# An output projection as three split products, its weights prepared during the recurrence and its low parts streamed in a ring

## The reference

```python
    o = group_rmsnorm(o, norm_g, HGRN_HEADS) * jax.nn.silu(g_out.astype(jnp.float32))   # recurrence
    ...
    return group_rmsnorm(b_gate * y, norm_g, CONV_GROUPS)                               # convolution
    ...
    h = h + jnp.concatenate([y_hgrn, y_conv], axis=-1) @ w_out[l]
    h = h + moe_ffn(rmsnorm(h, norm_ffn_g[l]), ...)
    return rmsnorm(h, norm_final_g)[:, N_META:]
```

## Time and profile before

| | us |
|---|---|
| three runs | 1575.82, 1578.70, 1580.32; median 1578.70 |
| the profiled execution | 1578.89 |
| its span, first to last instruction | 1577.1 |
| TensorE busy | 1492.2 (95%) |
| TensorE weight loads | 1273.3 |
| VectorE busy | 913.8 (58%) |
| GpSimd busy | 844.7 (54%) |
| ScalarE busy | 582.6 (37%) |
| granted TensorE clock, mean | 0.979 |

### The profile page before, as it was taken

How to read it: one execution, slowest core, us unless ns; L and a number is a source line. 1 busy time by engine, 2 the same in 40 slices (tenths; PEclk the granted TensorE clock), 3 DMA queues, 4 the chain that set the end, 5 groups by cost and what they waited for, 6 DMA issues and landing times.

```text
span 1577.1 us, 29085 instructions
## 1 busy us (share of the span) xinstructions
PE 1492.2 (95%) x9554; PEld 1273.3 (81%) x9554; DVE 913.8 (58%) x1595; ACT 582.6 (37%) x1052; POOL 844.7 (54%) x697
## 2 busy tenths in 40 slices
PE   6999999999979999979999999999999999999990
PEld 5799889899834666758999998888998998888980
DVE  3332688788867866344555546555555555555552
ACT  6433545444334321102333333333343333333333
POOL 0332163360601313335667877777777777777761
PEclk9999999999989999989999999999999999999995
DMA  5389521212070011426999999999999999999976
GB/s 189 92 261 299 196 80 31 76 53 80 28 287 27 28 54 54 161 78 246 334 326 339 333 328 325 328 328 344 339 336 326 335 327 325 331 320 340 327 213 229
DMA packets 104441, 356.95 MB, mean 226 GB/s; under 512 B 28151, under 2 KB 38360, under 8 KB 83406
## 3 DMA queue, kind: packets, MB, share of 16 engines
q1 hardware_dynamic: 60622, 246.60, 42.0%
q0 software_dynamic: 43776, 109.80, 26.2%
HBM read 300.68 MB, written 73.91 MB: 238 GB/s over the span
## 4 chain that ended last, share of the span: by engine, by line
PE 49%; DMA 3%; issue 1%; POOL 1%; ACT 0%; DVE 0%; POOLq 0%; SPq 0%; ACTq 0%
PE gu L1713 34%; PE ype L1735 4%; PE yrest L1724 4%; PE ype L1736 3%; PE ype L1737 3%; DMA acc_rows<-YE,sia 1%; DMA acc_rows<-YF,sib 1%; DMA A<-acc_rows 1%; POOL wi L1646 0%; POOL acc_rows L1653 0%; POOL acc_rows L1668 0%; DVE A L1892 0%; SPq L1627 0%; ACT junkf L1832 0%; ACT YF L1789 0%
## 5 line engine op out<-in xcount | busy, mean ns | idle before, releaser
L1646 POOL DMA_INDIRECT wi<-xn_rows,gi x320 | 412.7, 1290 | 117.1 <-issue 97.0
L1852 DVE TENSOR_TENSOR WL<-place,WH 128x2048 fp32r<-128x2048 f32 x65 | 149.1, 2294 | 329.9 <-ACT WH L1780 226.2
L1713 PEld LDWEIGHTS gu<-wi,place 128*128 128x128 f32 x2112 | 290.4, 190 | 5.9 <-issue 3.3
L1713 PE MATMUL gu<-wi,place 128*128 128x160 f32 x2112 | 293.0, 299 | 2.0 <-SPq L1609 1.9
L1713 PE MATMUL gu<-XS,place 128*128 128x160 f32 x2048 | 284.4, 299 | 1.7 <-issue 1.7
L1713 PEld LDWEIGHTS gu<-XS,place 128*128 128x128 f32 x2048 | 281.6, 190 | 5.1 <-issue 2.7
L1131 POOL DMA_INDIRECT slot_table<-pay,si x64 | 62.4, 975 | 170.6 <-DVEq L1440 155.0
L1653 POOL DMA_INDIRECT acc_rows<-YF,sib x65 | 107.1, 1648 | 76.3 <-ACT YF L1789 42.5
L1784 ACT ACTIVATE SS<-gu 128x160 f32<-128x160 f32 x130 | 39.3, 302 | 263.4 <-PE gu L1713 208.9
L1780 ACT ACTIVATE WH<-place 128x2048 fp32r<-128x2048 f32 x65 | 124.2, 1911 | 0.5 <-issue 0.5
L1668 POOL DMA_INDIRECT acc_rows<-YE,sia x65 | 102.8, 1581 | 33.6 <-issue 24.0
(11 more groups left out here) (299 smaller groups left out, 2717.2 us busy)
## 6 DMA issues: line engine op xcount, KB each, us to landing
place<-in_w_gate_e SPq DMA_DIRECT2D x65, 1024.0 KB
place<-in_w_up_e SPq DMA_DIRECT2D x65, 1024.0 KB
place<-in_w_down_e SPq DMA_DIRECT2D x65, 1024.0 KB
place<-in_w_in POOLq DMA_DIRECT2D x16, 512.0 KB, 7.2
late_parts<-wq_parts POOLq DMA_DIRECT2D x8, 1024.0 KB, 6.0
late_parts<-xn_parts POOLq DMA_DIRECT2D x8, 1024.0 KB, 6.0
wf_parts<-late_parts POOLq DMA_DIRECT2D x8, 1024.0 KB, 5.1
w_low<-late_parts POOLq DMA_DIRECT2D x8, 1024.0 KB, 5.2
```

Source lines behind the costliest of these rows:

```text
L1646: pool.indirect_dma_start(XQ[q][:, s * DQ:(s + 1) * DQ], None, quarters_d, bass.IndirectOffsetOnAxis(ap=index[s], axis=0), bounds_check=QU ...
L1713: last = pe.matmul(gu[f][:, k, :], raw[:, t, f * P:f * P + P], XS[q][:, t, :], start=(t == 0), stop=(t == KT - 1))
L1852: tt(WL[q][:, :], WR[q][2][:, :], WH[q][:, :].bitcast(F32), ALU.subtract).then_inc(s_dlo, 1)
```

## The change

`project` multiplies split operands: for each of the four chunks of a part, high rows by high weights, high rows by low weights, low rows by high weights, all in fp32r (three matmuls of 512 columns in the place of one in float32).

*The weights.* They are prepared in the recurrence, one chunk of 128 channels per turn. SyncE loads the chunk (512 KB). ScalarE multiplies it by the norm's gain per channel (`wo_chunk`) and rounds one half of its columns to fp32r behind `decays(3)`, the other behind the copy of the turned keys (`wo_high_part`). GpSimd subtracts (`wo_low_part`): for the first half of chunk 2h ahead of the convolution's first half of head h, for the second half ahead of its second, for chunk 2h + 1 behind the head's last step and at the start of the next head. SyncE stores both parts to DRAM (4 of 256 KB per chunk), and the next chunk's load waits for the subtractions of the one before. The stage's end waits for the last store.

*In the output stage.* The high weights stay in SBUF, loaded in two halves. The low weights come in 128 loads of one chunk and half, 256 KB each, in the order in which `project` uses them (`UNITS`), into a ring of 6 buffers; SyncE issues the first six between the two high halves, and a later one when the product that used its buffer is done. Up to the sixth chunk of the next tile they stand ahead of the wait for a tile's normed rows on SyncE's queue.

*The rows.* `mix` no longer multiplies by the gains. It writes the products into R, ScalarE copies them to fp32r (`conv_high`, `gated_high`), and VectorE subtracts: for the convolution within `mix`, for the recurrence's rows in the new `mixed`, which stands ahead of `residual`. `conv_high` stands behind the squares of the tile after next, `gated_high` behind that tile's roots and the kept transposes.

*Beside that.* The transposed rows xT keep 5 tiles instead of 8, so `keep` waits for the shared expert from tile 5 on; the squares of `row_squares` are written to X2 instead of a buffer of their own, behind waits for its last readers; in the router's tail and in the experts several counting semaphores are merged into one.

```diff
     K.QO = keep("QO", [P, HEADS, T])
+    K.GL, K.QH = (w[:, :, :].rearrange("p t n -> p (t n)").rearrange("p (h t) -> p h t", h=HEADS) for w in (WI0, WI1))
+    split = K.WQ[:, :, :].rearrange("p k n -> p (k n)")
+    K.YH = split[:, 0:HEADS * ALL].rearrange("p (c t) -> p c t", t=ALL)[:, :, META:ALL]
+    at = 2 * HEADS * ALL + 2 * D
+    K.YL = split[:, at:at + D].rearrange("p (i h t) -> p i h t", i=2, h=HEADS)
     K.V = K.place[:, 0:HEADS * ALL].rearrange("p (c t) -> p c t", t=ALL)
...
         tbl_rows = tbl_d.rearrange("(i c) w -> i (c w)", c=CAP)
+        s_ow, s_oh = sem("wo_chunk_in"), sem("wo_chunk_scaled_high")
+        s_ol, s_ost = sem("wo_chunk_low"), sem("wo_chunk_stored")
+        wo_raw, wo_hi, wo_lo = XN[:, 0, :], XP[:, 1, 0:HW], XP[:, 1, HW:2 * HW]
+        gains = K.ng[:, :, :].rearrange("p k h -> p (k h)")
...
+            sp.wait_ge(s_ps[1], 32 * HEADS)
+            for c in range(KT):
+                if c:
+                    sp.wait_ge(s_ol, 2 * c)
+                sp.dma_start(wo_raw, w_out[:, c, :]).then_inc(s_ow, 16)
+                for half in range(2):
+                    sp.wait_ge(s_ol, 2 * c + half + 1)
+                    sp.dma_start(K.wo_high_d[:, c, HW * half:HW * half + HW], wo_hi.bitcast(F32)).then_inc(s_ost, 16)
+                    sp.dma_start(K.wo_low_d[:, half, c, :], wo_lo.bitcast(F32)).then_inc(s_ost, 16)
+            sp.wait_ge(s_ost, 32 + 64 * KT)
...
+
+            def wo_low_part(c, half):
+                pool.wait_ge(s_oh, 3 * c + half + 2)
+                pool.tensor_tensor(wo_lo, wo_raw[:, HW * half:HW * half + HW], wo_hi.bitcast(F32), ALU.subtract).then_inc(s_ol, 1)
...
                 load_parts(h, 2)
+                if h:
+                    wo_low_part(2 * h - 1, 1)
                 for k in range(2):
+                    wo_low_part(2 * h, k)
...
+                wo_low_part(2 * h + 1, 0)
...
             def turn(h, r, ahead):
                 i = h * 2 + r
                 base = h * 10 + (FQ + 6 * r)
+
+                def wo_chunk():
+                    act.wait_ge(s_ow, i * 16 + 16)
+                    act.sem_inc(s_t, 1)
+                    act.activation(wo_raw, wo_raw, ACT.Copy, scale=gains[:, bass.ds(i, 1)]).then_inc(s_oh, 1)
+                    act.wait_ge(s_oh, i * 3 + 1)
+                    act.sem_inc(s_t, 1)
+
+                def wo_high_part(half):
+                    act.wait_ge(s_ost, i * 64 + (32 + 32 * half))
+                    act.sem_inc(s_t, 1)
+                    act.activation(wo_hi, wo_raw[:, HW * half:HW * half + HW], ACT.Copy).then_inc(s_oh, 1)
 
...
                 decays(3)
+                wo_chunk()
+                wo_high_part(0)
...
+                wo_high_part(1)
...
 
+        UNITS = [(half, HEADS * (1 - part) + h) for j in range(TT)
+                 for half, part in (((0, 0), (1, 0), (0, 1), (1, 1)) if j == 0 else ((0, 0), (0, 1), (1, 0), (1, 1)))
+                 for h in range(HEADS)]
+        PER_TILE = 4 * HEADS
...
         @block.sync
         def _(sp):
+            def load_low(u):
+                half, c = UNITS[u]
+                if u >= RING:
+                    sp.wait_ge(s_lu, u - RING + 1)
+                sp.dma_start(K.LO[:, u % RING, :].bitcast(F32), K.wo_low_d[:, half, c, :]).then_inc(s_lw[u % RING], 16)
+
             for k in range(2):
-                sp.dma_start(wo[:, :, 512 * k:512 * k + 512], w_out[:, :, 512 * k:512 * k + 512]).then_inc(s_wo[k], 16)
+                sp.dma_start(WO[:, :, 512 * k:512 * k + 512].bitcast(F32), K.wo_high_d[:, :, 512 * k:512 * k + 512]).then_inc(s_wo[k], 16)
+                if k == 0:
+                    for u in range(RING):
+                        load_low(u)
             sp.dma_start(H[0], x[:, 0, :]).then_inc(s_h[0], 16)
...
             for j in range(TT):
+                for u in range(j * PER_TILE + RING, min((j + 1) * PER_TILE + RING, len(UNITS))):
+                    load_low(u)
...
                         pe.wait_ge(s_wo[half], 16)
-                rows = slice(j * P, j * P + P)
+                rows, cols = slice(j * P, j * P + P), slice(512 * half, 512 * half + 512)
                 for h in range(HEADS):
-                    c, y = (h, K.QO) if part else (HEADS + h, YC)
-                    last = pe.matmul(op[half][:, :], y[:, h, rows], wo[:, c, 512 * half:512 * half + 512],
-                                     start=(part == 0 and h == 0), stop=(part == 1 and h == HEADS - 1))
+                    u = done["chunks"]
+                    c = h if part else HEADS + h
+                    assert UNITS[u] == (half, c)
+                    high = (K.QH if part else K.YH)[:, h, rows]
+                    low = K.GL[:, h, rows] if part else K.YL[:, j % 2, h, :]
+                    pe.matmul(op[half][:, :], high, WO[:, c, cols], start=(part == 0 and h == 0), stop=False)
+                    pe.wait_ge(s_lw[u % RING], 16 * (u // RING + 1))
+                    pe.matmul(op[half][:, :], high, K.LO[:, u % RING, :], start=False, stop=False).then_inc(s_lu, 1)
+                    last = pe.matmul(op[half][:, :], low, WO[:, c, cols], start=False, stop=(part == 1 and h == HEADS - 1))
+                    done["chunks"] += 1
...
+                if j >= KEPT:
+                    act.wait_ge(s_gu, j - KEPT + 1)
                 for k in range(2):
-                    last = act.copy(K.xT[:, 4 * k:4 * k + 4, j * P:j * P + P], td[k][:, :, :])
+                    last = act.copy(xT_of(j)[:, 4 * k:4 * k + 4, :], td[k][:, :, :])
                 last.then_inc(s_e2, 1)
...
-                act.activation(junk, H[j % NH], ACT.Square, accum_out=sh[:, j:j + 1]).then_inc(s_s2, 1)
+                if j >= 2:
+                    act.wait_ge(s_t2, j - 1)
+                    act.wait_ge(s_xw[j % 2], 16 * (j // 2))
+                act.activation(X2[j % 2], H[j % NH], ACT.Square, accum_out=sh[:, j:j + 1]).then_inc(s_s2, 1)
...
 
+            def conv_high(j):
+                act.wait_ge(s_mx, 2 * j + 1)
+                act.activation(K.YH[:, :, j * P:j * P + P], R[j % 2][:, HEADS:2 * HEADS, :], ACT.Copy).then_inc(s_mh, 1)
+
+            def gated_high(j):
+                act.wait_ge(s_mx, 2 * j + 2)
+                act.activation(K.QH[:, :, j * P:j * P + P], R[j % 2][:, 0:HEADS, :], ACT.Copy).then_inc(s_mh, 1)
+
...
             for j in range(TT):
                 if j + 2 < TT:
                     squares(j + 2)
+                if j + 1 < TT:
+                    conv_high(j + 1)
+                if j + 2 < TT:
                     roots(j + 2)
                 if j >= 1:
                     keep(j - 1)
+                if j + 1 < TT:
+                    gated_high(j + 1)
                 row_squares(j)
...
                 step(nc.vector.reciprocal(conv, conv))
-                for h in range(HEADS):
-                    last = stt(YC[:, h, cols], YC[:, h, cols], K.ng[:, 1, h:h + 1], conv[:, h, :], ALU.mult, ALU.mult)
-                last.then_inc(s_y, 1)
+                step(tt(conv, conv, YC[:, :, cols], ALU.mult))
+                dve.sem_inc(s_mx, 1)
                 step(nc.vector.reciprocal(gated, gated))
+                dve.wait_ge(s_mh, 2 * j + 1)
+                if j >= 2:
+                    dve.wait_ge(s_op, 2 * j - 2)
+                tt(K.YL[:, j % 2, :, :], conv, K.YH[:, :, cols].bitcast(F32), ALU.subtract).then_inc(s_y, 1)
                 dve.wait_ge(s_sig, j + 1)
                 step(tt(gated, gated, sg[j % 2], ALU.mult))
-                for h in range(HEADS):
-                    last = stt(G[:, h, cols], G[:, h, cols], K.ng[:, 0, h:h + 1], gated[:, h, :], ALU.mult, ALU.mult)
-                step(last)
-                tt(K.QO[:, :, cols], K.QO[:, :, cols], G[:, :, cols], ALU.mult).then_inc(s_y, 1)
+                step(tt(gated, gated, G[:, :, cols], ALU.mult))
+                step(tt(gated, gated, K.QO[:, :, cols], ALU.mult))
+                dve.sem_inc(s_mx, 1)
+
+            def mixed(j):
+
+                gated, cols = R[j % 2][:, 0:HEADS, :], slice(j * P, j * P + P)
+                dve.wait_ge(s_mh, 2 * j + 2)
+                tt(K.GL[:, :, cols], gated, K.QH[:, :, cols].bitcast(F32), ALU.subtract).then_inc(s_y, 1)
...
                     shared_hidden(j - LAG - 1)
+                if j + 1 < TT:
+                    mixed(j + 1)
...
-                        sp.sem_inc(turn["sp"], 1)
+                        sp.sem_inc(s_turn, 1)
                         sp.wait_ge(s_yr, n - 1)
-                        sp.sem_inc(turn["sp"], 1)
```

109 lines of the change are left out of this document (64 added, 45 removed).

## The result

The changed kernel took 1609.0 us (median of four runs, 1606.8 to 1609.9) beside 1579.1 us of the kernel before: ratio 1.0193, interval 1.0171 to 1.0216, so 30 us slower. The forecast was 1596 (1583 to 1611). Sign and main cause were right; the size was 13 us short, and the stretch from tile 4 to the end, forecast as a gain of 8.3 us, came out as a loss of 4.5.

The account below looks back on a forecast made before the run. TensorE was taken to set the output stage's pace in tiles 4 to 7, VectorE in tiles 1 to 3. Recurrence 4.9, stores 0.5, start 16.4, mix 3.8, products -8.3 make +17.3 on 1578.9: 1596 us, range 1583 to 1611.

Parts of the forecast that it names:

- The named wait: Output stage, tile 0: TensorE idle 12 to 15 us for a DMA of wo_low, clock 0.50 behind it.
- tile 1 to hidden(0): Output stage up to the shared expert's first hidden rows: VectorE's longer mix in tiles 1 to 3, +3.8 us.
- hidden(0) to the end: From the shared expert's first hidden rows on: cheaper products in tiles 4 to 7, less one new wait, -8.3 us.
- The late w_low: Recurrence: GpSimd's subtraction delays each head's convolution and the w_low load queued behind it, +4.9 us over four heads.
- The 0.5 us for the last stores: Recurrence's end: the last chunk's stores end just behind the stage's end, +0.5 us.
- The start: Output stage, tile 0: the seventh low chunk lands behind queued loads, then half clock; tile 1 restarts at 487.8, +16.4 us.
- lies inside this wait: Output stage's start: the first part starts 3.7 us later behind VectorE's second reciprocal, hidden in the seventh chunk's wait.
- Inside a burst of eight the ring keeps up: Output stage: a 0.26 MB low load takes 0.66 us against 0.70 of use per unit, so nothing added.
- about 4 us in tile 1 and 1 in tile 3: Output stage: TensorE stands still because SyncE waits for normed rows; beside VectorE's later chain, so nothing added.
- the ring starves in every tile: Output stage rival: low loads cost SyncE over 1 us each, +7; or VectorE is slowed; 1603 to 1611, chance 0.13.
- The gain of the products: Output stage, tiles 4 to 7: each projection part saves 0.56 us, 9.0 in all, less 0.7: -8.3 us.
- The mix: Output stage, VectorE: 1.5 us more per tile over tiles 1 to 3, less 0.7: +3.8 us; covered in tiles 4 to 7.

Follow-up runs that it names:

- d: Changed kernel with x rows and shared weights issued one at a time between the ring's refills, not ahead of them: 1597.2 us, ratio 1.0118 to the kernel before.
- b: Changed kernel without the output-weight preparation in the recurrence, raw weights standing where the parts would: 1609.1 us, ratio 1.0197 to the kernel before.
- j: h with the second high half issued behind four low units, not ten, and without the weight preparation: 1562.8 us, ratio 0.9973 to the kernel before.
- l: h with the second high half behind four low units and the wait for the last stores at the output stage's head: 1564.3 us, ratio 0.9994.
- c: Changed kernel with one fp32 product of the high parts for the three fp32r products, no low parts loaded: 1595.8 us, ratio 1.0099 to the kernel before.
- g: Changed kernel with d's issue order, e's ring of ten, and ScalarE's roots and keep ahead of conv_high: 1579.7 us, ratio 1.0016 to the kernel before.
- h: g with two low-part subtractions moved on VectorE: tile 0's conv half before the second reciprocal, the next tile's gated half behind the residual: 1575.3 us, ratio 0.9995.
- e: Changed kernel with a ring of ten low units instead of six, xT keeping three tiles instead of five: 1593.4 us, ratio 1.0104 to the kernel before.
- a: Changed kernel loading only the first six low units, products reading whatever lies in their slot: 1584.7 us, ratio 1.0045 to the kernel before.

## Why the prediction was partly right

**Direction and main cause: right.** The named wait came: 14.41 us for a DMA of wo_low in tile 0 (12 to 15 forecast), with the granted clock at 0.54 over the stretch, and tile 1's first product at 492.6 (near 493 forecast). d shows that the backlog makes the wait.

**The sum, term by term.** Forecast against trace, in us:

| step | forecast | measured |
|---|---|---|
| recurrence, to the stage's start | +5.4 | +3.1 in the trace; 2 to 3 by b and j |
| stage's start to tile 1's first product | +16.4 | +18.2 |
| tile 1 to hidden(0) | about +3.8 | +4.4 |
| hidden(0) to the end | about -8.3 | +4.5 |
| sum | +17.3 | +30.2 |

**The late w_low: wrong, 4.9 us too much.** The step "The convolution started at 328.87; now 0.56 + 1.06 + 0.14 + 0.62 + 0.15 + 1.31 + 0.1 behind the decay of 329.69" took the wrong decay. ScalarE's row at 329.69 is two decays behind the one that the new calls follow, which ran at 324.41 in the changed kernel. GpSimd was free by then, so its subtraction was done at 328.8, and TensorE has no wait for w_low in the recurrence of the changed kernel. The 0.5 us for the last stores did not come either: the stage follows the state update, as l shows. What the preparation does cost, 2 to 3 us, comes through VectorE, which the sum had at 0 and the upper bound at 7. That the total of the recurrence looks nearly right (+3.1 for +5.4) is luck: one term that did not come stands in for one that was put at 0.

**The start: right in its mechanism**, 1.8 us small. That VectorE's second reciprocal "lies inside this wait" held in the changed kernel, but only there: with the wait gone it is on the path, as c, g and h show.

**"Inside a burst of eight the ring keeps up": wrong, and this is the step that failed.** It compared a unit's 0.66 us of transfer with 0.70 of use, a rate, and left out how long a freed slot stays empty. From the end of a low product to the next use of its slot, six units of 0.70 less the product's own 0.39 are 3.8 us; a load issued at once needs 3.7. So the ring just keeps up when every load is issued at once, and has no room for a late one. Ten short waits (10.7 us) and the clock behind them took what the products gained. The wait behind the normed rows was forecast too ("about 4 us in tile 1 and 1 in tile 3", put at nothing beside VectorE's chain) and came as 2.64 us in tile 1. By the marks: hidden(0) to hidden(4) takes 115.6 us in the changed kernel, 103.0 in e and 109.7 before. A ring of ten gives 12.6 us back in that stretch alone (7.7 against the 110.7 us of b, which has the same stage as the changed kernel). The rival "the ring starves in every tile" had the place right. Its reason, over 1 us for each issue so that a burst runs at SyncE's pace, is seen only in places (in tile 4 three issues stand 1.4 us apart, from 577.43 on, with all their slots free by 576.9), and its chance of 0.13 was too small.

**The gain of the products: right in size.** 8.3 us were forecast; a against c gives 7.0 (marks) to 8.5 (ratios). Part of it, 1.3 us, lies ahead of hidden(0), where the sum had none. It was there, and the ring spent it.

**The mix: undersized.** 3.8 us were forecast; c gives 9.4. The missing part is the start, where 4.2 us more lie between means(0) and the first product (13.25 in c, 9.02 before), which the forecast had hidden inside the ring's wait. Nothing was added from tile 4 on, as forecast.

**How the terms add up.** At hidden(4): stage's start +3.2, mix +9.4, products -7.0, ring +26.0, sum +31.6. They are differences along one chain of kernels (before, c, a, changed), so they must add up, and the sum is no proof of their sizes. Of the ring's 26.0, e against a gives 10.9 to the backlog, and the changed kernel against e the other 15.1 to the six slots. The split depends on the order in which the two are taken away: by the ratios, d takes 11.8 us away and leaves 11.5 for the slots, while e takes 14.0 away and leaves 9.3 for the backlog. The end is 1.4 us less late than hidden(4); no experiment was aimed at that.

## What to carry to other kernels

A ring's rate is not its service: count for a burst how many units are used before the first freed slot is filled again, with some room for a load that is issued late, and compare that with the depth; here six slots lost what ten kept. Ask of each refill what stands in front of it in its queue, and issue what is not needed soon in between, not ahead. And when a term is hidden inside another's wait, it is not gone: once the larger one is mended, it is the next one to pay. Another queue for the low parts was not tried; the Trainium skill ("DMA: Bandwidth & Descriptors", Queues, rings and completion order) says that each DMA engine takes the queues that have work in turn, packet by packet, which no run here shows.
